# Streaming both halves of x as one 512-column operand in the recurrent block's weight slots

## Chip, core and metric

The kernel runs on one core of one Trainium2 chip. The metric is the device time of one execution in microseconds; the kernel before takes 2019.62 us (median of 3 runs, 2018.29 to 2022.55). The engines are TensorE (PE, its weight loads shown as PEld), VectorE (DVE), ScalarE (ACT), GpSimd (POOL) and SyncE (SP), which issues the transfers. Each works through its own instructions in order and they meet only at semaphores.

## The reference, cut to what matters

Two layers of one kind follow a first block; the change lies in the first block's recurrent part, where x is 256 tokens by 2048 features and `w_in` has 2048 columns for `u_lru` and 2048 for `g_lru`.

```python
xn = rms_norm(x, norm_pre_w[l])
z = xn @ w_in[l]
u_lru, g_lru, q, k, v, g_attn, m_lru, m_attn = jnp.split(z, split_at, axis=-1)
u = centred_depthwise_conv(u_lru, conv_w[l], conv_b[l])      # 4 taps along the tokens
h = rg_lru(u, ..., False) + rg_lru(u, ..., True)
y_a = h * jax.nn.silu(g_lru)

def rg_lru(u, w_r, b_r, w_i, b_i, lam, reverse):             # 16 blocks of 128 features
    gate_r = sigmoid(einsum(u, w_r) + b_r)
    gate_i = sigmoid(einsum(u, w_i) + b_i)
    log_a = -LRU_C * gate_r * softplus(-lam)
    a = exp(log_a)
    b = sqrt(-expm1(2.0 * log_a)) * (gate_i * u)
    return associative_scan over tokens of h = a * h + b
```

## The kernel before

All matrices arrive as "slots" of 128 x 2048 numbers (1 MB each). A slot n passes three stages in the class `Ring`: SP loads it into one of two raw buffers (`load`, L251), ACT rounds it to the short format fp32r (`round`, L260, the instruction at L267), DVE subtracts the rounded from the raw weights to get the residual (`residual`, L269, the instruction at L274). `w_hi` and `w_lo` have four places each. A raw buffer is loaded anew once the residual of the slot that held it is done; a place of `w_hi` is overwritten once PE has counted the slot as `used`. x is likewise held as `xn_hi` and `xn_lo`. A product is three matmuls: hi·hi, lo·hi and hi·lo.

Slots 0 to 31 are the recurrent part. `features` (L294) multiplies one slot, that is 128 output features over all 2048 inputs: for each of 16 rows kk it issues three matmuls with 256 moving columns (the tokens), 48 in all, adding up in the left half of one of the four PSUM banks `z0` to `z3`. The pass i (L1107 to L1117) takes slots 4i and 4i+1 (two tiles of u, banks 0 and 1), slots 4i+2 and 4i+3 (two tiles of g, banks 2 and 3), and then `gates(i)` (L1095), the 8 small products of the gate matrices with the convolved u. There are 8 passes. Slots 32 to 39 follow (keys and values, `tokens`, L306, with 512 moving columns), then the attention part.

Beside PE, ACT and DVE each run a loop that is written out by hand (ACT L599 to L627, DVE L859 to L888). Its iteration i serves the gates and the scan of pass i-1 and the convolution of pass i. With n = 4i:

- ACT: `gate_inputs(i-1)` takes the sigmoid of the two g tiles from PSUM (L555), `gates(i-1)` takes 8 sigmoids of the gate products (L563, L565), then round n+3, 4 tanh (L575), round n+4, two `input_copy` of u out of PSUM into `padded` (L593), 4 exp (L582), a square root (L585), rounds n+5 and n+6, and `round_y` (L597), which waits for DVE's y.
- DVE: `open_gates(i-1)` (L829: g times its sigmoid, from PSUM), residual n+3, residual n+4, `convolve` of two tiles (each L818 and three of L822, each waiting for the one before), the scan (L835 to L844), residual n+5, `outputs_lru` (L849 and L852, the instruction that writes y), residual n+6 and `split_y` (L856).
- POOL multiplies gate_i by u (L509) as soon as the 8 sigmoids are done.

PE starts a u slot of pass i when `input_copy` of pass i-1 has emptied its bank (`ucopied`), a g slot when `open_gates` of pass i-1 has (`zcopied`), and `gates(i)` when both convolutions of pass i are done (`conv`). In iteration 0 DVE works through a chain of small instructions for the angles and for softplus (L163 to L173, L892 to L896) before it comes to `open_gates(0)`.

Of the kernel before, what the change touches and what calls it, by code (L numbers as in the profile page):

```python
# [10 lines left out]
F32R = mybir.dt.float32r  # L11
I32 = mybir.dt.int32
ACT = mybir.ActivationFunctionType
ALU = mybir.AluOpType
AX_X = mybir.AxisListType.X

P = 128
D = 2048
T = 256
KT = D // P  # L20
# [4 lines left out]
SLOTS = 4  # L25
# [6 lines left out]
LRU_PASSES = KT // 2  # L32
# [211 lines left out]
class Ring:  # L244
# [49 lines left out]
    def features(self, pe, n, out, x_hi, x_lo, each=None, whole=True):  # L294
# [8 lines left out]
                ins = pe.matmul(out, w[:, kk], x[:, kk], start=kk == 0 and j == 0, stop=kk == KT - 1 and j == 2)  # L303
        ins.then_inc(self.s.used, 1)

    def tokens(self, pe, n, quarter, outs, x_hi, x_lo):  # L306

        w_hi, w_lo = (w[:, n % SLOTS].rearrange("p (k f) -> p k f", k=4) for w in (self.k.w_hi, self.k.w_lo))
        self.await_slot(pe, n)
        for kk in range(4):  # L310
            row = 4 * quarter + kk
            for m in range(2):
                t = slice(P * m, P * m + P)
                for j, (x, w) in enumerate(((x_hi, w_hi), (x_hi, w_lo), (x_lo, w_hi))):
                    ins = pe.matmul(outs[m], x[:, row, t], w[:, kk], start=row == 0 and j == 0, stop=row == KT - 1 and j == 2)  # L315
        ins.then_inc(self.s.used, 1)
# [26 lines left out]
def reduce_angles(link, dve, angle, turns, rest, looked):  # L343
# [4 lines left out]
    for n, quarter in enumerate((0.0, 0.25)):  # L348
# [5 lines left out]
        for m, part in enumerate(turn_parts):  # L354
# [5 lines left out]

B1_SEMS = ("loaded0 loaded1 rounded split used "
           "p1_in ident_in consts_in x0 x1 x2 x3 eps squared averaged rooted first0 first1 first2 first_rounded first_split scaled ascaled turned xrounded xsplit "
           "weights0 weights1 gated cleared chain exped ucopied conv gsig zcopied gates taken decay dsteps rounded_y ydone "
           "counted rotary_in rchain rlooked mask_in sink_in sinkready "
           "kcopied kroped kturned keyed vcopied qcopied roped qturned qevac scored0 scored1 soft0 soft1 "
           "exped0 exped1 flipped0 flipped1 fcopied0 fcopied1 mixed0 mixed1 yout0 yout1 yrounded0 yrounded1 ylo silued "
# [4 lines left out]
def first_block(k, t):  # L371

    nc = k.nc
    z, aux = k.z, k.aux
    with phase(nc, "b1", B1_SEMS) as s:
        put, goto = k.put, k.goto
        ring = Ring(k, s, 0, 0, SLOTS_1 + SLOTS - 1)
# [6 lines left out]
        padded = put("padded", [P, 2, T + 4])  # L384
        gsig, g_all, y = put("gsig", [P, 2, T]), put("g_all", [P, 2, T]), put("y", [P, 2, T])
        gate_r, gate_i, decay, tau = (put(n, [P, 2, 2, T]) for n in ("gate_r", "gate_i", "decay", "tau"))
# [47 lines left out]
        soft, exped = (s.soft0, s.soft1), (s.exped0, s.exped1)  # L434
# [5 lines left out]

        def tile(n):
            return z[n][:, 0:T]

        def pair(c):
            return (z[2 * (c % 2)][:, 0:Q], z[2 * (c % 2) + 1][:, 0:Q])
# [10 lines left out]
        with nc.Block() as block:  # L456
# [55 lines left out]
            def _(act):  # L512
# [34 lines left out]
                ring.round(act, 1)  # L547
                ring.round(act, 2)

                def gate_inputs(i):  # L550
                    act.wait_ge(s.used, 4 * i + 4)
                    if i:
                        act.wait_ge(s.zcopied, 2 * i)
                    for b in range(2):
                        act.activation(gsig[:, b], tile(2 + b), ACT.Sigmoid).then_inc(s.gsig, 1)  # L555

                def gates(i):
                    if i:
# [40 lines left out]
                for i in range(LRU_PASSES + 1):  # L599
                    n = 4 * i  # L600
                    if i:
                        gate_inputs(i - 1)
                        gates(i - 1)
                    ring.round(act, n + 3)
                    if i:
                        tanhs(i - 1)
                    ring.round(act, n + 4)
                    if i < LRU_PASSES:
                        input_copy(i, 0)
                        input_copy(i, 1)  # L610
                    if i:
                        exps_lru(i - 1)
                    else:
                        act.wait_ge(s.chain, 2)
                        act.activation(tmp[1][:], tmp[0][:], ACT.Exp).then_inc(s.exped, 1)
                    ring.round(act, n + 5)
                    if i == 0:

                        act.wait_ge(s.rchain, RCHAIN_1 + 8)
                        act.activation(sin_1[:, :, 0:16], rest_1[:, :, 0:16], ACT.Sin, scale=-1.0).then_inc(s.rlooked, 1)  # L620
                        act.activation(sin_1[:, :, 16:32], rest_1[:, :, 16:32], ACT.Sin).then_inc(s.rlooked, 1)
                    ring.round(act, n + 6)
                    if i == 0:
                        act.wait_ge(s.rchain, RCHAIN_1 + 16)
                        act.activation(cos_1[:], rest_1[:], ACT.Sin).then_inc(s.rlooked, 1)
                    if i:
                        round_y(i - 1)  # L627
# [141 lines left out]
            def _(dve):  # L769
# [41 lines left out]

                def convolve(i, b):
                    dve.wait_ge(s.ucopied, 2 * i + b + 1)
                    u = u_all[:, 2 * i + b:2 * i + b + 1]
                    for tap in range(4):
                        x = padded[:, b, tap:tap + T]
                        if tap == 0:
                            ins = dve.tensor_scalar(u, x[:, None], col(P1_CONV, 2 * i + b), col(P1_CONVB, 2 * i + b),  # L818
                                                    ALU.mult, ALU.add)
                        else:  # L820
                            dve.wait_ge(s.conv, 8 * i + 4 * b + tap)
                            ins = dve.scalar_tensor_tensor(out=u, in0=x[:, None], scalar=col(P1_CONV + 16 * tap, 2 * i + b),  # L822
                                                           in1=u, op0=ALU.mult, op1=ALU.add)
                        ins.then_inc(s.conv, 1)

                def open_gates(i):
                    dve.wait_ge(s.gsig, 2 * i + 2)
                    for b in range(2):
                        dve.tensor_tensor(g_all[:, b], tile(2 + b), gsig[:, b], ALU.mult).then_inc(s.zcopied, 1)  # L829

                def scan(i):
                    def step(n):
# [26 lines left out]
                for i in range(LRU_PASSES + 1):  # L859
                    n = 4 * i  # L860
                    if i:
                        open_gates(i - 1)
                    ring.residual(dve, n + 3)
                    if i == 0:
                        link = chain(dve, s.chain)
                        link(lambda: dve.tensor_scalar(rate[:], params[:, P1_LAM:P1_LAM + 32], -1.0, None, ALU.mult))
# [203 lines left out]
            def _(pe):  # L1070
# [36 lines left out]
                for i in range(LRU_PASSES):  # L1107
                    for b in range(2):
                        if i:
                            pe.wait_ge(s.ucopied, 2 * (i - 1) + b + 1)  # L1110
                        first = i == b == 0
                        ring.features(pe, 4 * i + b, tile(b), k.xn_hi, k.xn_lo, first_rows if first else None, not first)
                    for b in range(2):
                        if i:
                            pe.wait_ge(s.zcopied, 2 * (i - 1) + b + 1)
                        ring.features(pe, 4 * i + 2 + b, tile(2 + b), k.xn_hi, k.xn_lo)
                    gates(i)  # L1117

                pe.wait_ge(s.ucopied, 2 * LRU_PASSES)
                for w in range(4):  # L1120
                    ring.tokens(pe, SLOT_K + w, w, pair(0), k.xn_hi, k.xn_lo)

# [7 lines left out]
                        if h % 2:  # L1130
                            ins.then_inc(out_sem, 1)

                pe.wait_ge(s.zcopied, 2 * LRU_PASSES)
                for w in range(4):
                    ring.tokens(pe, SLOT_V + w, w, pair(1), k.xn_hi, k.xn_lo)
                    if w == 1:
# [1704 lines left out]
def build(nc, t):  # L2841

    with ExitStack() as stack:
# [17 lines left out]
        k.cos_t, k.sin_t = put("cos_t", [P, T]), put("sin_t", [P, T])  # L2861
        k.xn_at = SBUF_END - 8 * KT * T
        k.middle = goto(k.xn_at)
        k.xn_hi, k.xn_lo = (put(n, [P, KT, T], F32R) for n in ("xn_hi", "xn_lo"))
        goto(k.xn_at)
        k.junk = put("junk", [P, D])
        goto(k.xn_at + 4 * KT * T)
# [107 lines left out]
```

## Time and profile before

| what | value |
|---|---|
| median of 3 runs | 2019.62 us |
| the profiled execution | 2015.25 us |
| its span (first to last instruction) | 2013.5 us |
| PE busy in the span | 1942.0 us |
| DVE busy | 1265.4 us |
| ACT busy | 1099.0 us |
| granted TensorE clock, mean | 0.990 |

The profiled execution is 4.37 us below the median and 1.75 us longer than its span. Each row of a timeline gives the start, the duration, the engine, the line, the operation with its output and inputs, and, in brackets, the idle time of the engine before it with what ended it. Rows of one line that follow each other are merged (x4). Matmuls overlap in their records, so their pace is read from the distance of the starts and not from the durations.

### The profile page before, as it was taken

Reading aid. Unit: us, or ns where it says so; the run is one execution under the profiler, and the core shown is the slowest. Engines: PE = TensorE matmul, PEld = TensorE weight load, DVE = VectorE, ACT = ScalarE, POOL = GpSimd, SP = SyncE. Lnnn points to the kernel's source line nnn. Section 1 sums busy time; section 2 is a strip of 40 time slices with the busy share of each in tenths; the row PEclk is TensorE's granted clock in tenths of the full one; section 3 lists DMA queues with packets and bytes.
Section 4 is the critical chain, followed back from the end, with each engine's and each line's share of the span. In section 5 each row is a group of like instructions: output and inputs, shape, how many; then the busy total and the mean of one; then the engine's idle time right before and its main releaser. Section 6 shows DMA issues by size and latency. Waiting matters only on the chain. (4 is left out here: it accounts for less than half of the span.)

```text
span 2013.5 us, 32797 instructions
## 1 busy us (share of the span) xinstructions
PE 1942.0 (96%) x13840; PEld 1731.8 (86%) x13840; DVE 1265.4 (63%) x1768; ACT 1099.0 (55%) x1499; POOL 70.0 (3%) x66
## 2 busy tenths in 40 slices
PE   6999999999999999999999999999989998999998
PEld 6999989999888888887898988888879998998886
DVE  5877755555444444654697878554547889765453
ACT  5877745554433333334655579626454656883451
POOL 0111100000000000000000101100000000010000
PEclk9999999999999999999999999999999999999999
DMA  6455454444455555464644333313655443342153
GB/s 219 186 189 186 152 205 162 160 147 147 167 189 194 194 182 201 173 249 146 236 163 174 135 129 126 126 65 126 212 185 197 178 147 126 126 147 85 65 208 127
DMA packets 52274, 328.63 MB, mean 163 GB/s; under 512 B 7968, under 2 KB 10144, under 8 KB 14368
## 3 DMA queue, kind: packets, MB, share of 16 engines
q1 hardware_dynamic: 52128, 326.54, 45.0%
q8 instruction: 109, 1.79, 0.3%
q14 instruction: 37, 0.30, 0.0%
HBM read 320.23 MB, written 6.29 MB: 162 GB/s over the span
## 5 line engine op out<-in xcount | busy, mean ns | idle before, releaser
L274 DVE TENSOR_TENSOR w_lo<-w_raw,w_hi 128x2048 fp32r<-128x2048 f32 x275 | 633.6, 2305 | 439.9 <-ACT w_hi L267 439.7
L267 ACT ACTIVATE w_hi<-w_raw 128x2048 fp32r<-128x2048 f32 x287 | 549.5, 1917 | 514.0 <-PE z L315 249.6
L303 PE MATMUL z<-xn_hi,w_hi 128*128 128x256 f32 x2112 | 621.0, 294 | 4.3 <-DVE w_lo L274 2.9
L303 PE MATMUL z<-xn_hi,w_lo 128*128 128x256 f32 x2112 | 598.0, 283 | 0.0
L303 PE MATMUL z<-xn_lo,w_hi 128*128 128x256 f32 x2112 | 597.4, 283 | 0.0
L303 PEld LDWEIGHTS z<-xn_hi,w_hi 128*128 128x128 f32 x2112 | 401.5, 190 | 20.7 <-issue 9.3
L303 PEld LDWEIGHTS z<-xn_lo,w_hi 128*128 128x128 f32 x2112 | 400.3, 190 | 5.1 <-issue 4.3
L303 PEld LDWEIGHTS z<-xn_hi,w_lo 128*128 128x128 f32 x2112 | 398.7, 189 | 0.0
L315 PE MATMUL z<-w_hi,xn_hi 128*128 128x512 f32 x568 | 226.9, 399 | 0.0
L315 PE MATMUL z<-w_lo,xn_hi 128*128 128x512 f32 x568 | 225.2, 396 | 0.0
L315 PE MATMUL z<-w_hi,xn_lo 128*128 128x512 f32 x568 | 225.1, 396 | 0.0
L315 PE MATMUL z<-w_hi,y_hi 128*128 128x512 f32 x368 | 143.6, 390 | 0.0
L315 PE MATMUL z<-w_hi,y_lo 128*128 128x512 f32 x368 | 143.3, 389 | 0.0
L315 PE MATMUL z<-w_lo,y_hi 128*128 128x512 f32 x368 | 143.2, 389 | 0.0
L315 PEld LDWEIGHTS z<-w_hi,xn_lo 128*128 128x128 f32 x568 | 107.0, 188 | 26.1
L315 PEld LDWEIGHTS z<-w_hi,xn_hi 128*128 128x128 f32 x568 | 107.0, 188 | 25.4
L315 PEld LDWEIGHTS z<-w_lo,xn_hi 128*128 128x128 f32 x568 | 107.0, 188 | 25.3
L1963 DVE SCALAR_TENSOR_TENSOR acc<-padded_b,params,acc 128x256 f32<-128x256 f32 x240 | 98.4, 478 | 0.0
L315 PEld LDWEIGHTS z<-w_hi,y_lo 128*128 128x128 f32 x368 | 69.1, 188 | 14.5
L315 PEld LDWEIGHTS z<-w_hi,y_hi 128*128 128x128 f32 x368 | 69.1, 188 | 14.1
L315 PEld LDWEIGHTS z<-w_lo,y_hi 128*128 128x128 f32 x368 | 69.1, 188 | 14.1
L2121 DVE SCALAR_TENSOR_TENSOR conv<-padded,params,conv 128x256 f32<-128x256 f32 x108 | 58.1, 538 | 35.2 <-ACT conv L1692 32.6
(425 smaller groups left out, 2525.0 us busy)
## 6 DMA issues: line engine op xcount, KB each, us to landing
w_raw<-in_w_dram SPq DMA_DIRECT2D x287, 1024.0 KB, 4.8
gate_w<-in_lru_w_dram SPq DMA_DIRECT2D x8, 512.0 KB, 5.3
x_t<-state_dram SPq DMA_DIRECT2D x2, 2048.0 KB, 7.8
x_first<-in_x_dram SPq DMA_DIRECT2D x4, 512.0 KB, 6.7
x_t<-in_x_dram SPq DMA_DIRECT2D x1, 2048.0 KB, 10.9
state_dram<-x_t SPq DMA_DIRECT2D x2, 1024.0 KB, 5.3
pw<-in_pw_dram SPq DMA_DIRECT2D x2, 1024.0 KB, 6.2
state_dram<-x_t SPq DMA_DIRECT2D x8, 256.0 KB, 2.1
```

The source lines that it names most:

```text
L267: act.activation(self.k.w_hi[:, n % SLOTS], self.k.w_raw[:, m % RAW], ACT.Copy).then_inc(self.s.rounded, 1)
L274: dve.tensor_tensor(self.k.w_lo[:, n % SLOTS], self.k.w_raw[:, m % RAW], self.k.w_hi[:, n % SLOTS].bitcast(F32), ALU.subtract).then_inc(se ...
L303: ins = pe.matmul(out, w[:, kk], x[:, kk], start=kk == 0 and j == 0, stop=kk == KT - 1 and j == 2)
L315: ins = pe.matmul(outs[m], x[:, row, t], w[:, kk], start=row == 0 and j == 0, stop=row == KT - 1 and j == 2)
L1963: dve.scalar_tensor_tensor(out=acc[:, b], in0=padded_b[:, b, n:n + T], scalar=col(w), in1=acc[:, b], op0=ALU.mult, op1=ALU.add).then_inc(s ...
L2121: dve.scalar_tensor_tensor(out=conv[:, i], in0=padded[:, i, tap:tap + T], scalar=col(w), in1=conv[:, i], op0=ALU.mult, op1=ALU.add).then_i ...
```

## The change

The 32 slots use a new function `wide_features`. `xn_hi` and `xn_lo` are now two halves of one tensor `xn` of shape [128, 2, 16, 256]. For each row kk, `w_hi` is loaded once and multiplied with both halves of x as one moving operand of 512 columns (two runs of 256), giving hi·hi in the left half of the bank and lo·hi in the right half; `w_lo` with `xn_hi` is added to the left half. A slot has 32 matmuls where it had 48. The sum of the halves is made outside: ACT copies the left half to SBUF, DVE adds the right half from PSUM. For u the copy is the `input_copy` that was there and the addition is new in `convolve`; for g the copy (`take_gates`) and the addition (`join_gates`) are both new, and the sigmoid and the product with it now read `g_all` in SBUF. PE waits for the additions (`ujoined`, `gjoined`) instead of `ucopied` and `zcopied`.

```diff
+    def wide_features(self, pe, n, out, x, each=None, whole=True):
+        w_hi, w_lo = (w[:, n % SLOTS].rearrange("p (k f) -> p k f", k=KT) for w in (self.k.w_hi, self.k.w_lo))
+        parts = out[:, 0:2 * T].rearrange("p (b t) -> p b t", b=2)
+        if whole:
+            self.await_slot(pe, n)
+        for kk in range(KT):
+            if each is not None:
+                each(kk)
+            if kk < KT - 1:
+                pe.matmul(parts, w_hi[:, kk], x[:, :, kk], start=kk == 0, stop=False)
+            ins = pe.matmul(out[:, 0:T], w_lo[:, kk], x[:, 0, kk], start=False, stop=False)
+            if kk == KT - 1:
+                ins = pe.matmul(parts, w_hi[:, kk], x[:, :, kk], start=False, stop=True)
+        ins.then_inc(self.s.used, 1)
...
+                def take_gates(i):
+                    act.wait_ge(s.used, 4 * i + 4)
+                    if i:
+                        act.wait_ge(s.dsteps, 8 * i)
+                    for b in range(2):
+                        act.activation(g_all[:, b], tile(2 + b), ACT.Copy).then_inc(s.gtaken, 1)
                 def gate_inputs(i):
-                    act.wait_ge(s.used, 4 * i + 4)
...
-                        act.activation(gsig[:, b], tile(2 + b), ACT.Sigmoid).then_inc(s.gsig, 1)
+                        act.wait_ge(s.gjoined, 2 * i + b + 1)
+                        act.activation(gsig[:, b], g_all[:, b], ACT.Sigmoid).then_inc(s.gsig, 1)
...
                     if i:
+                        take_gates(i - 1)
+                        gates(i - 1)
                         gate_inputs(i - 1)
-                        gates(i - 1)
                     ring.round(act, n + 3)
...
                 def convolve(i, b):
                     dve.wait_ge(s.ucopied, 2 * i + b + 1)
+                    inner = padded[:, b, 2:2 + T]
+                    dve.tensor_tensor(inner, rest(b), inner, ALU.add).then_inc(s.ujoined, 1)
+                    dve.wait_ge(s.ujoined, 2 * i + b + 1)
...
+                def join_gates(i):
+                    for b in range(2):
+                        dve.wait_ge(s.gtaken, 2 * i + b + 1)
+                        dve.tensor_tensor(g_all[:, b], rest(2 + b), g_all[:, b], ALU.add).then_inc(s.gjoined, 1)
...
                     if i:
+                        join_gates(i - 1)
+                    ring.residual(dve, n + 3)
+                    if i:
                         open_gates(i - 1)
-                    ring.residual(dve, n + 3)
...
                         if i:
-                            pe.wait_ge(s.ucopied, 2 * (i - 1) + b + 1)
+                            pe.wait_ge(s.ujoined, 2 * (i - 1) + b + 1)
                         first = i == b == 0
-                        ring.features(pe, 4 * i + b, tile(b), k.xn_hi, k.xn_lo, first_rows if first else None, not first)
+                        ring.wide_features(pe, 4 * i + b, z[b], k.xn, first_rows if first else None, not first)
```

On PE, within a slot of pass 1, the rows were:

```order
L1103 MATMUL aux<-u_all,gate_w_85 128x256 x8
L303 MATMUL z<-xn_hi,w_hi 128x256
L303 MATMUL z<-xn_lo,w_hi 128x256
L303 MATMUL z<-xn_hi,w_lo 128x256
L303 MATMUL z<-xn_hi,w_hi 128x256
```

(the number behind a name is its buffer's) and are now, at the end of one slot and the start of the next:

```order
L316 MATMUL z<-xn,w_hi 128x512
L317 MATMUL z<-xn,w_lo 128x256 x2
L319 MATMUL z<-xn,w_hi 128x512
L316 MATMUL z<-xn,w_hi 128x512
L317 MATMUL z<-xn,w_lo 128x256
```

Two matmuls of 256 columns on the same weights have become one of 512; in the last row the order of the two is turned round.

On DVE, one iteration from y to the scan (L274 is a residual, L829 `open_gates`, L818 and L822 `convolve`) was:

```order
L852 TENSOR_TENSOR y<-gate_r,g_all 128x512
L274 TENSOR_TENSOR w_lo<-w_raw,w_hi 128x2048
L856 TENSOR_TENSOR y_lo<-y,y_hi 128x512
L829 TENSOR_TENSOR g_all<-z,gsig 128x256 x2
L274 TENSOR_TENSOR w_lo<-w_raw,w_hi 128x2048 x2
L818 TENSOR_SCALAR u_all<-padded,params 128x256
L822 SCALAR_TENSOR_TENSOR u_all<-padded,params,u_all 128x256 x3
L818 TENSOR_SCALAR u_all<-padded,params 128x256
L822 SCALAR_TENSOR_TENSOR u_all<-padded,params,u_all 128x256 x3
```

and is now (L859 `join_gates`, L865 `open_gates`, L842 the addition in `convolve`):

```order
L888 TENSOR_TENSOR y<-gate_r,g_all 128x512
L274 TENSOR_TENSOR w_lo<-w_raw,w_hi 128x2048
L892 TENSOR_TENSOR y_lo<-y,y_hi 128x512
L859 TENSOR_TENSOR g_all<-z,g_all 128x256 x2
L274 TENSOR_TENSOR w_lo<-w_raw,w_hi 128x2048
L865 TENSOR_TENSOR g_all<-g_all,gsig 128x256 x2
L274 TENSOR_TENSOR w_lo<-w_raw,w_hi 128x2048
L842 TENSOR_TENSOR padded<-z,padded 128x256
L848 TENSOR_SCALAR u_all<-padded,params 128x256
L852 SCALAR_TENSOR_TENSOR u_all<-padded,params,u_all 128x256 x3
L842 TENSOR_TENSOR padded<-z,padded 128x256
L848 TENSOR_SCALAR u_all<-padded,params 128x256
```

Four instructions of 256 columns are added, and `open_gates` has moved behind residual n+3.

On ACT, from `round_y` to round n+3 (L267), the rows were:

```order
L597 ACTIVATE y_hi<-y 128x512
L555 ACT_TABLE_LOAD
L555 ACTIVATE gsig<-z 128x256 x2
L563 ACTIVATE gate_r<-aux,params 128x256
L565 ACTIVATE gate_i<-aux,params 128x256
```

and are now:

```order
L623 ACTIVATE y_hi<-y 128x512
L574 ACTIVATE g_all<-z 128x256 x2
L589 ACT_TABLE_LOAD
L589 ACTIVATE gate_r<-aux,params 128x256
```

The two copies are added, and the two `gsig` (now L581) have moved behind the 8 sigmoids, ahead of round n+3.

## Rows read from the trace of the kernel before

**Rows 1.** The page: busy time of the engines.
```profile
PE 1942.0 (96%) x13840; PEld 1731.8 (86%) x13840; DVE 1265.4 (63%) x1768; ACT 1099.0 (55%) x1499; POOL 70.0 (3%) x66
```

**Rows 2.** Timeline of PE, slot 31 into gates(7): start, duration, instruction.
```profile
227.83 0.29 PE L303 MATMUL z<-xn_hi,w_lo 128*128 128x256 f32 x1
...
233.71 2.54 PE L1103 MATMUL aux<-u_all,gate_w 128*128 128x256 f32 x11
```

**Rows 3.** Timeline of PE, a stretch of 512-column matmuls.
```profile
699.79 0.39 PE L315 MATMUL z<-w_hi,xn_hi 128*128 128x512 f32 x1
...
705.88 0.40 PE L315 MATMUL z<-w_hi,xn_lo 128*128 128x512 f32 x1
```

**Rows 4.** Timeline of PE: gates(1), gates(2).
```profile
74.78 3.62 PE L1103 MATMUL aux<-u_all,gate_w 128*128 128x256 f32 x16
...
101.28 3.62 PE L1103 MATMUL aux<-u_all,gate_w 128*128 128x256 f32 x16
```

**Rows 5.** Timeline of DVE, iteration 3.
```profile
105.25 0.69 DVE L852 TENSOR_TENSOR y<-gate_r,g_all 128x512 f32<-128x512 f32 x1
...
113.33 2.94 DVE L274 TENSOR_TENSOR w_lo<-w_raw,w_hi 128x2048 fp32r<-128x2048 f32 x1 [3.91 <-ACT w_hi L267]
116.72 2.29 DVE L274 TENSOR_TENSOR w_lo<-w_raw,w_hi 128x2048 fp32r<-128x2048 f32 x1 [0.45 <-ACT w_hi L267]
118.93 0.41 DVE L818 TENSOR_SCALAR u_all<-padded,params 128x256 f32<-128x256 f32 x1
119.38 1.52 DVE L822 SCALAR_TENSOR_TENSOR u_all<-padded,params,u_all 128x256 f32<-128x256 f32 x3
...
122.70 1.22 DVE L835 SCALAR_TENSOR_TENSOR tau<-decay,tau 128x1024 f32<-128x1024 f32 x1
...
126.41 0.67 DVE L842 TENSOR_TENSOR_SCAN gate_r<-decay,tau 128x256 f32<-128x256 f32 x1
...
130.55 0.69 DVE L852 TENSOR_TENSOR y<-gate_r,g_all 128x512 f32<-128x512 f32 x1
```

**Rows 6.** Timeline of ACT, iteration 3.
```profile
105.98 0.63 ACT L597 ACTIVATE y_hi<-y 128x512 fp32r<-128x512 f32 x1 [4.35 <-DVE y L852]
...
114.72 1.97 ACT L267 ACTIVATE w_hi<-w_raw 128x2048 fp32r<-128x2048 f32 x1
...
121.57 1.06 ACT L585 ACTIVATE tau<-tau 128x1024 f32<-128x1024 f32 x1
```

**Rows 7.** Timeline of POOL, same iteration.
```profile
111.57 2.55 POOL L509 TENSOR_TENSOR gate_i<-gate_i,u_all 128x512 f32<-128x512 f32 x2 [22.74 <-ACT gate_i L565]
```

**Rows 8.** Timelines of ACT and DVE, iteration 1.
```profile
66.01 0.62 ACT L593 ACTIVATE padded<-z 128x256 f32<-128x256 f32 x2
66.65 1.28 ACT L582 ACT_TABLE_LOAD   x1
...
62.69 0.75 DVE L829 TENSOR_TENSOR g_all<-z,gsig 128x256 f32<-128x256 f32 x2
63.35 2.28 DVE L274 TENSOR_TENSOR w_lo<-w_raw,w_hi 128x2048 fp32r<-128x2048 f32 x1
```

**Rows 9.** Timeline of PE: three idle stretches, in brackets.
```profile
27.11 0.58 PE L303 MATMUL z<-xn_hi,w_hi 128*128 128x256 f32 x1 [2.89 <-DVE w_lo L274]
...
63.16 0.38 PE L303 MATMUL z<-xn_hi,w_hi 128*128 128x256 f32 x1 [0.90 <-DVE g_all L829]
...
1157.29 0.33 PE L2518 MATMUL aux<-ident,S 128*128 128x128 f32 x1 [2.06 <-DVE S L2102]
```

**Rows 10.** Windows: PE, PEld, DVE, ACT, POOL busy; granted clock; DMA share, GB/s.
```profile
30.00:33.00 3.00, 3.00 (x16) 3.00 (x15) 1.08 (x1) 0.00 (x0) 0.00 (x0) 0.50 0.86 350
1155.00:1160.00 5.00, 2.94 (x19) 1.73 (x19) 2.53 (x9) 4.97 (x8) 0.00 (x0) 1.00 0.54 203
```

**Rows 11.** Timeline of DVE, iterations 7 and 8.
```profile
236.05 0.69 DVE L852 TENSOR_TENSOR y<-gate_r,g_all 128x512 f32<-128x512 f32 x1
...
257.80 2.27 DVE L274 TENSOR_TENSOR w_lo<-w_raw,w_hi 128x2048 fp32r<-128x2048 f32 x1
```

More of the change, by code:

```diff
@@ L362 @@
            "p1_in ident_in consts_in x0 x1 x2 x3 eps squared averaged rooted first0 first1 first2 first_rounded first_split scaled ascaled turned xrounded xsplit "
-           "weights0 weights1 gated cleared chain exped ucopied conv gsig zcopied gates taken decay dsteps rounded_y ydone "
+           "weights0 weights1 gated cleared chain exped ucopied ujoined conv gtaken gjoined gsig zcopied gates taken decay dsteps rounded_y ydone "
            "counted rotary_in rchain rlooked mask_in sink_in sinkready "
@@ L442, in tile, with rest @@
             return z[n][:, 0:T]
+        def rest(n):
+            return z[n][:, T:2 * T]
         def pair(c):
@@ L824, in convolve @@
                         ins.then_inc(s.conv, 1)
+                def join_gates(i):
+                    for b in range(2):
+                        dve.wait_ge(s.gtaken, 2 * i + b + 1)
+                        dve.tensor_tensor(g_all[:, b], rest(2 + b), g_all[:, b], ALU.add).then_inc(s.gjoined, 1)
                 def open_gates(i):
                     dve.wait_ge(s.gsig, 2 * i + 2)
+                    dve.wait_ge(s.gjoined, 2 * i + 2)
                     for b in range(2):
-                        dve.tensor_tensor(g_all[:, b], tile(2 + b), gsig[:, b], ALU.mult).then_inc(s.zcopied, 1)
+                        dve.tensor_tensor(g_all[:, b], g_all[:, b], gsig[:, b], ALU.mult).then_inc(s.zcopied, 1)
                 def scan(i):
@@ L1109, in _ @@
                         if i:
-                            pe.wait_ge(s.ucopied, 2 * (i - 1) + b + 1)
+                            pe.wait_ge(s.ujoined, 2 * (i - 1) + b + 1)
                         first = i == b == 0
-                        ring.features(pe, 4 * i + b, tile(b), k.xn_hi, k.xn_lo, first_rows if first else None, not first)
+                        ring.wide_features(pe, 4 * i + b, z[b], k.xn, first_rows if first else None, not first)
                     for b in range(2):
                         if i:
-                            pe.wait_ge(s.zcopied, 2 * (i - 1) + b + 1)
-                        ring.features(pe, 4 * i + 2 + b, tile(2 + b), k.xn_hi, k.xn_lo)
+                            pe.wait_ge(s.gjoined, 2 * (i - 1) + b + 1)
+                        ring.wide_features(pe, 4 * i + 2 + b, z[2 + b], k.xn)
                     gates(i)
-                pe.wait_ge(s.ucopied, 2 * LRU_PASSES)
+                pe.wait_ge(s.ujoined, 2 * LRU_PASSES)
                 for w in range(4):
@@ L1131, in turn_heads @@
                             ins.then_inc(out_sem, 1)
-                pe.wait_ge(s.zcopied, 2 * LRU_PASSES)
+                pe.wait_ge(s.gjoined, 2 * LRU_PASSES)
                 for w in range(4):
@@ L2863, in build @@
         k.middle = goto(k.xn_at)
-        k.xn_hi, k.xn_lo = (put(n, [P, KT, T], F32R) for n in ("xn_hi", "xn_lo"))
+        k.xn = put("xn", [P, 2, KT, T], F32R)
+        k.xn_hi, k.xn_lo = k.xn[:, 0], k.xn[:, 1]
         goto(k.xn_at)
```

## The prediction

> **What bounds the kernel now.** I read the page first: PE is busy in 96% of the span [rows 1], so what counts is its pace and its few waits. From 227.83 to 233.71 PE starts 49 matmuls of 256 columns, one per 0.1200 us, so a slot of 48 takes 5.76 us [rows 2]. With 512 columns 26 starts take 6.09 us, 0.2342 us each [rows 3]. gates(1) and gates(2) start 26.50 us apart [rows 4]; less 4 x 5.76 that leaves 3.45 us for the gate products. In the passes after the first PE has one idle stretch, 0.90 us at slot 6 [rows 9]. So PE bounds the stage. Before pricing anything I looked at how much room ACT and DVE have behind it, because the change gives both of them work.
>
> They have less than their busy shares suggest, because they form a loop. DVE writes y; ACT has waited for it (4.35 us idle), does round_y, the gate sigmoids and round n+3; DVE has waited for that (3.91 us idle), and then works almost without a pause through two residuals, the convolutions, the scan and residual n+5 to the next y [rows 5, 6]. From y to y this takes 130.55 - 105.25 = 25.30 us, and nothing in it waits for PE. That is 1.2 us less than PE's pass. The loop started late (softplus in iteration 0) and gains 1.2 us per pass until it meets PE: y of iteration 7 comes at 236.05 [rows 11], 26.4 us per pass after that of iteration 3, PE's own pace.
>
> **The change part by part.**
>
> *PE.* A wide slot has 16 x 0.2342 + 16 x 0.1200 = 5.667 us against 5.760: 0.093 us less. The number of streamed columns is the same (768 per row kk); all that goes is what a matmul costs beyond its columns, 2 x 0.1200 - 0.2342 = 0.0058 us, 16 times. Slot 0 is fed row by row by x and slot 1 runs largely at half clock, where there is nothing to win if the two sizes scale with the columns; 30 slots give 2.8 us. A pass becomes 4 x 5.667 + 3.45 = 26.12 us. Bounds: the wide operand has two runs of 256 columns, which no row shows; at worst it costs two matmuls (0.240, nothing saved). At best the whole 0.0133 us per small matmul above 256 columns at 2.4 GHz (0.1067) is a fixed price paid once: 0.2267, 0.21 us per slot, 6.4 us. I take 0.2342, the measured operand of that size.
>
> By the Trainium skill (TensorE: Matmul & The Clock Gate, back-to-back rates of a warm array) a matmul starts N/2.4 + 2.5 ns after the one before, which would make the saving an estimated 16 x 2.5 = 40 ns per slot; the rows are at 120 and 234 ns where the rule has 109 and 216, so the trace does not agree.
>
> *The ACT/DVE loop, what it gains in length.* (a) The two copies of take_gates stand on the chain from y to round n+3. Two such copies cost 66.65 - 66.01 = 0.64 us [rows 8]. The two gsig only change places within that chain. So round n+3 and everything behind it on ACT is 0.64 later. (b) join_gates falls into DVE's 3.91 us of idle: nothing. (c) open_gates now stands between the two residuals, about 0.66 us on DVE (62.69 to 63.35 in [rows 8]). Residual n+3 took 2.94 us where the next took 2.29; POOL runs from 111.57 to 114.12 [rows 7] and residual n+3 starts at 113.33, inside. Now it starts 0.64 later against POOL, at 113.97, and nearly all of the 0.65 of stretching goes. It ends at about 116.36 as before (116.27), open_gates reaches 117.02, and residual n+4 waits for ACT's round n+4 anyway: 114.72 + 0.64 + 2.00 = 117.36, against 116.72. So (a) to (c) together move residual n+4 by 0.64. If the stretching stayed, DVE would be the later one, by 0.15: that is the bound above. (d) Each convolution gets an addition that its first tap waits for. The nearest row is L818, same width, waited for by the next: 119.38 - 118.93 = 0.45; read from PSUM, L829 has 0.33 for each of an unchained pair [rows 8]. I take 0.44, 0.88 for two. Bounds: 0.33 and the scan's 0.67 [rows 5]. The square root that the scan needs ended at 122.63 with the scan at 122.70 [rows 5, 6]; it moves by 0.64, the scan by 1.52, so nothing is added there. The loop becomes 25.30 + 0.64 + 0.88 = 26.82 us.
>
> The Trainium skill (SBUF, who interferes with whom) calls the port pair of VectorE and GpSimd an exclusive lock against which a two-input VectorE instruction fully blocks; the 2.94 us of residual n+3 agrees with that.
>
> So the loop, now faster than PE by 1.2 us per pass, becomes slower than PE by 0.7. The rest is a matter of where each starts.
>
> *Where they meet.* In iteration 0 the two additions delay DVE by 0.88; its chain up to the sinks, and so join_gates(0), starts at 62.69 + 0.88 = 63.57. PE may start slot 6 when the first addition is done, about 64.03 instead of 63.16. PE would be there at 62.26 - 4 x 0.093 = 61.88, so it idles 2.15 us instead of 0.90: 1.25 us lost. Two wide slots later gates(1) is at 64.03 + 11.33 + 0.1 = 75.46 (before: 74.78). Residual 7 starts at 63.35 + 0.88 = 64.23 [rows 8], takes 2.2, open_gates 0.66, so residual 8 starts at 67.1. From there to the scan, which starts as the convolutions end, it was 122.70 - 116.72 = 5.98 [rows 5], now 6.86: they end at 74.0, ahead of PE by 1.5. From here DVE's end of the convolutions runs at 26.82 per pass: 100.8, 127.6, 154.5, 181.3, 208.1, 234.9. PE at 26.12 asks for gates(2) at 101.6, gates(3) at 127.7 and gates(4) at 153.8. From gates(4) on PE waits, about 0.7 us in each of four passes. gates(7) starts at 235.0 against 233.71 [rows 2]: 1.3 us later.
>
> *Behind the stage.* DVE goes into the key and value slots late. y of iteration 7 came at 236.05, 7.85 us behind the scan's start, and moves to 242.7 (+6.7); residual n+5 of iteration 8, slot 37, ended at 257.80 + 2.27 = 260.07 [rows 11] and moves by 6.7 + 0.64 to 267.4. PE wants slot 37 at 235.0 + 3.45 + 5 x 24 x 0.2342 = 266.5. It waits 0.9 us; the key transposes behind slot 37 may add 0.1. After that ACT and DVE have little beside the weights, and the ring catches up; the shift of PE reaches the end, since PE stays the bound.
>
> *The sum.* -2.8 (30 slots) + 1.25 (slot 6) + 4 x 0.7 (gates) + 1.0 (slot 37) = +2.25, less roundings: +2.2 us. The profiled execution of 2015.25 would become 2017.5; against the median of 2019.62 that is 2021.8 us.
>
> **Rivals.**
>
> *A. PE bounds throughout, not slower than before.* The loop stays at or below 26.1, because the additions pipeline (0.33 each) and the copies hide: 25.30 + 0.66 = 25.96. For: DVE still idles 3.9 us per pass. Against: that idle time is a wait inside the loop, not room. Price: -2.8 + 1.2 at slot 6, -1.6: 2018.0 us.
>
> *B. Slower by over 0.2%: the additions in convolve cost as much as the scan's 0.67.* They read PSUM and write in place over data that the tap waits for. Each is then 0.23 dearer, 0.46 per pass, counted in iteration 0 and in six loops: +3.2 on top of +2.2, so 2025.0 us. It decides from 0.57 us per addition (1.8 us / 14 more). Against: L818, also waited for, has 0.45. Late weight transfers in the lengthened loop would look alike.
>
> *C. The wide matmul saves nothing (0.240).* PE's pass stays at 26.49 and gates(1) comes at 75.65, then PE is at 234.6 for gates(7), still before the loop's 235.0. The time is the forecast's, 2021.8: from pass 4 on the loop decides, and the pace of the matmul does not matter. For the same reason the best case of 0.2267 gains only at the start, under 1 us.
>
> *D. The idle 2.15 us at slot 6 lowers the clock.* After 2.89 us of idle the granted clock was 0.50 at 30 to 33 us, the 1.2 GHz level [rows 9, 10]. After 2.06 us at 1157 the window around it is granted 1.00. If it falls as it did then (27.11 to 33, 5.9 us at half pace), PE loses some 3 us at slots 6 and 7, but the loop is behind by then and gates(7) is still set by it: under 0.5 us more. The sum stays.
>
> **How the numbers follow.** Forecast, with C and D (they end at the same time): 0.68. A: 0.10. B or a like lengthening: 0.18. Something that makes both PE and the loop faster: 0.04. What a measurement of this kernel can tell from no change is about 0.2%, 4 us. Over 4 us faster needs a gain beyond the best bound of the matmul at an unchanged loop: 0.04. Over 4 us slower is B and the upper end of the forecast: 0.22. Within: 0.74. The range: A with its spread and the runs' scatter of 2 us gives 2017.5 below; B beyond its middle gives 2026.5.
>
> **What would show it.** Wide matmuls start 0.234 apart and the small ones 0.120; y to y is 26.8 us on DVE from iteration 1 on; PE idles 2.1 us before slot 6, nothing before gates(2) and gates(3), 0.7 us before gates(4) to gates(7) (released by u_all, DVE), and 0.9 before slot 37; residual n+3 falls to about 2.3 us. I am wrong if PE has no waits before the gates (then A) or if they exceed 1.2 us each (then B).

## The result, and the profile after

The changed kernel takes 2023.67 us (median of 22 runs, 2019.98 to 2030.24) against 2019.95 us for the kernel before (22 runs, 2015.33 to 2023.40). The ratio is 1.0021, 95% interval 1.0014 to 1.0029: 4.2 us slower, between 2.8 and 5.9 (the two medians alone differ by 3.7). The profiled execution took 2022.95 us and has a span of 2020.9. The forecast was 2.2 us slower. The direction and the length of the loop came out; the size was about half of what was measured, because a wait at the start of the stage was overlooked.

First the starts of the gate products on PE in the changed kernel, and PE's waits around them (start, duration, instruction; in brackets the idle time and what ended it; the same instructions as in [rows 4] and [rows 9]):

```profile
46.42 3.72 PE L1141 MATMUL aux<-u_all,gate_w 128*128 128x256 f32 x16 [0.40 <-DVE u_all L852]
63.93 0.50 PE L316 MATMUL z<-xn,w_hi 128*128 128x512 f32 x1 [2.57 <-DVE g_all L859]
76.94 3.72 PE L1141 MATMUL aux<-u_all,gate_w 128*128 128x256 f32 x16
103.77 3.72 PE L1141 MATMUL aux<-u_all,gate_w 128*128 128x256 f32 x16 [0.67 <-DVE u_all L852]
130.60 3.72 PE L1141 MATMUL aux<-u_all,gate_w 128*128 128x256 f32 x16 [0.68 <-DVE u_all L852]
...
237.93 3.72 PE L1141 MATMUL aux<-u_all,gate_w 128*128 128x256 f32 x16 [0.68 <-DVE u_all L852]
270.32 0.50 PE L331 MATMUL z<-w_hi,xn 128*128 128x512 f32 x1 [0.56 <-DVE w_lo L274]
```

From gates(2) on, and not only from gates(4) as forecast, PE waits in every pass for the second convolution, and the gates come 26.83 us apart where they came 26.49 apart. gates(7) is at 237.93 instead of 233.71. Next DVE, one iteration of its loop (the rows that answer to [rows 5]):

```profile
111.47 0.69 DVE L888 TENSOR_TENSOR y<-gate_r,g_all 128x512 f32<-128x512 f32 x1
...
120.17 2.34 DVE L274 TENSOR_TENSOR w_lo<-w_raw,w_hi 128x2048 fp32r<-128x2048 f32 x1 [4.53 <-ACT w_hi L267]
122.43 0.75 DVE L865 TENSOR_TENSOR g_all<-g_all,gsig 128x256 f32<-128x256 f32 x2
123.56 2.29 DVE L274 TENSOR_TENSOR w_lo<-w_raw,w_hi 128x2048 fp32r<-128x2048 f32 x1 [0.38 <-ACT w_hi L267]
125.77 0.42 DVE L842 TENSOR_TENSOR padded<-z,padded 128x256 f32<-128x256 f32 x1
126.22 0.41 DVE L848 TENSOR_SCALAR u_all<-padded,params 128x256 f32<-128x256 f32 x1
...
130.46 1.22 DVE L871 SCALAR_TENSOR_TENSOR tau<-decay,tau 128x1024 f32<-128x1024 f32 x1
```

y of the next iteration starts at 138.30, 26.83 after this one. An addition costs 126.22 - 125.77 = 0.45 us. Residual n+3 takes 2.34 us and no longer 2.94, and open_gates fits into the wait ahead of the next residual. The loop is the forecast's to 0.01 us.

Then the place where the forecast did not hold. ACT in iteration 1, the wait for the gate additions:

```profile
63.91 0.75 ACT L581 ACTIVATE gsig<-g_all 128x256 f32<-128x256 f32 x2 [5.29 <-DVE g_all L859]
64.57 1.90 ACT L267 ACTIVATE w_hi<-w_raw 128x2048 fp32r<-128x2048 f32 x1
```

ACT has finished its 8 sigmoids at 58.6 and stands idle for 5.29 us, because gsig needs the joined g, and join_gates(0) on DVE comes at 63.46, behind the softplus chain. Round 7, which stands behind gsig, starts at 64.57. Residual 7 on DVE starts at 66.49 instead of the forecast's 64.23.

Last the pace of the matmuls within a wide slot of the changed kernel:

```profile
108.03 0.39 PE L316 MATMUL z<-xn,w_hi 128*128 128x512 f32 x1
108.26 0.28 PE L317 MATMUL z<-xn,w_lo 128*128 128x256 f32 x1
108.38 0.39 PE L316 MATMUL z<-xn,w_hi 128*128 128x512 f32 x1
...
110.83 0.39 PE L316 MATMUL z<-xn,w_hi 128*128 128x512 f32 x1
```

Seven rows kk (110.83 less 108.38) take 2.45 us, 0.350 each: 0.23 for the wide matmul and 0.12 for the small one. A slot of 16 rows takes 5.60 us, 0.16 less than before, where the forecast had 0.09.

### The profile page after: what moved, and what is told of

Its sections match the earlier page's. It is cut to its first block and busy times, and to the rows that moved or that the text cites. A ratio compares the mean times of both kernels' runs of the same rounds, so it can differ in the third digit from the quotient of the medians.

```text
span 2020.9 us, 31839 instructions
## 1 busy us (share of the span) xinstructions
PE 1942.5 (96%) x13328; PEld 1706.0 (84%) x13328; DVE 1273.9 (63%) x1800; ACT 1103.7 (55%) x1515; POOL 70.4 (3%) x66
## 5 line engine op out<-in xcount | busy, mean ns | idle before, releaser
L274 DVE TENSOR_TENSOR w_lo<-w_raw,w_hi 128x2048 fp32r<-128x2048 f32 x275 | 629.6, 2290 | 442.3 <-ACT w_hi L267 442.0
L267 ACT ACTIVATE w_hi<-w_raw 128x2048 fp32r<-128x2048 f32 x287 | 549.0, 1915 | 519.2 <-PE z L331 240.4
L303 PE MATMUL z<-xn,w_hi 128*128 128x256 f32 x3200 | 606.4, 289 | 1.1 <-DVE xn L232 1.1
L303 PEld LDWEIGHTS z<-xn,w_hi 128*128 128x128 f32 x3200 | 497.8, 190 | 22.2 <-issue 14.2
L303 PE MATMUL z<-xn,w_lo 128*128 128x256 f32 x1600 | 452.4, 283 | 0.0
L331 PE MATMUL z<-w_hi,xn 128*128 128x512 f32 x1136 | 363.5, 398 | 0.6 <-DVE w_lo L274 0.6
L303 PEld LDWEIGHTS z<-xn,w_lo 128*128 128x128 f32 x1600 | 301.4, 188 | 0.0
L331 PEld LDWEIGHTS z<-w_hi,xn 128*128 128x128 f32 x1136 | 214.0, 188 | 52.4 <-DVE w_lo L274 1.0
L331 PE MATMUL z<-w_lo,xn 128*128 128x512 f32 x568 | 225.2, 396 | 0.0
L316 PE MATMUL z<-xn,w_hi 128*128 128x512 f32 x480 | 176.0, 405 | 5.4 <-DVE w_lo L274 2.9
L317 PE MATMUL z<-xn,w_lo 128*128 128x256 f32 x512 | 139.3, 282 | 0.0
L331 PEld LDWEIGHTS z<-w_lo,xn 128*128 128x128 f32 x568 | 107.0, 188 | 25.3
L316 PEld LDWEIGHTS z<-xn,w_hi 128*128 128x128 f32 x480 | 91.7, 191 | 26.5 <-DVE w_lo L274 3.2
L317 PEld LDWEIGHTS z<-xn,w_lo 128*128 128x128 f32 x512 | 97.9, 191 | 2.7
```

Source lines behind the costliest of these rows:

```text
L267: act.activation(self.k.w_hi[:, n % SLOTS], self.k.w_raw[:, m % RAW], ACT.Copy).then_inc(self.s.rounded, 1)
L274: dve.tensor_tensor(self.k.w_lo[:, n % SLOTS], self.k.w_raw[:, m % RAW], self.k.w_hi[:, n % SLOTS].bitcast(F32), ALU.subtract).then_inc(se ...
L316: pe.matmul(parts, w_hi[:, kk], x[:, :, kk], start=kk == 0, stop=False)
L317: ins = pe.matmul(out[:, 0:T], w_lo[:, kk], x[:, 0, kk], start=False, stop=False)
```

## The experiments

Because the start of the stage differs between profiles (gates(0) lies between 45.5 and 47.4 us, slot 1 starting when its weights are there and running partly at the lower clock), the table gives the distance from gates(0) to gates(7), read like the rows above. In the kernels whose gates(0) waits for DVE (changed, narrow, early_join, early_take, both, and by 0.21 us noadd) this distance starts at DVE's first convolutions; in the kernel before these ended at 45.4 us, and gates(0) came later, at 47.13, for PE's own sake. Ratios are to the kernel before, run anew beside each. The distances come from one profiled execution each, the ratios from all runs. The column of y is the distance of two y on DVE in iterations 1 to 4.

| kernel | gates(0) | gates(1) less gates(0) | gates(7) less gates(0) | y to y | ratio, 95% interval |
|---|---|---|---|---|---|
| before | 47.13 | 27.65 | 186.58 | 25.30 | 1 |
| changed | 46.42 | 30.52 | 191.51 | 26.83 | 1.0021 (1.0014 to 1.0029) |
| narrow | 47.41 | 30.51 | 191.45 | 26.82 | 1.0014 (1.0005 to 1.0023) |
| noadd | 45.63 | 30.59 | 185.91 | 25.30 | 0.9985 (0.9975 to 0.9995) |
| early_join | 47.28 | 28.20 | 189.19 | 26.83 | 1.0010 (1.0001 to 1.0019) |
| early_take | 46.85 | 30.51 | 190.22 | 26.28 | 1.0007 (0.9997 to 1.0016) |
| both | 47.15 | 28.20 | 185.86 | 26.28 | 1.0000 (0.9990 to 1.0010) |
| weave_only | 46.29 | 28.97 | 184.41 | 25.88 | 0.9988 (0.9979 to 0.9997) |
| woven | 45.48 | 26.75 | 182.18 | 25.33 | 0.9967 (0.9956 to 0.9977) |
| narrow_woven | 46.96 | 26.44 | 185.06 | 25.33 | 0.9976 (0.9967 to 0.9985) |

(From y of iteration 3 to that of 4 it is 26.04 in the kernel before and 26.54 in noadd; the other early intervals of these two are 25.30. In the kernel before, ACT there waits 0.68 us for PE's u, the first sign of PE's pace in the loop; in noadd it waits 1.13 us for late weights.)

**narrow: the additions without the wide matmul.**

```diff
-            if kk < KT - 1:
-                pe.matmul(parts, w_hi[:, kk], x[:, :, kk], start=kk == 0, stop=False)
+            if kk == 0:
+                pe.matmul(parts, w_hi[:, kk], x[:, :, kk], start=True, stop=False)
+            elif kk < KT - 1:
+                for half in range(2):
+                    pe.matmul(out[:, half * T:half * T + T], w_hi[:, kk], x[:, half, kk], start=False, stop=False)
```

> The changed kernel, but in the 14 inner rows kk of each slot the 512-column matmul is two of 256 columns again (the second into the right half of the bank); copies and additions stay. Theory (from gates(2) on the ACT/DVE loop of 26.83 us sets the pace, not the matmuls): gates(7) starts at 237.9 us as in the changed kernel, PE's waits before the gates shrink from 0.68 to about 0.35 us, y to y stays 26.8, time within 0.5 us of the changed kernel's, 4 to 5 us above before. Rival (matmul pace counts): each pass 0.33 us longer, gates(7) at 240 or later.

The distances are those of the changed kernel (191.45 against 191.51). The ratios, 1.0014 and 1.0021, have overlapping intervals; the time is 2.8 us above before, where 4 to 5 was expected. gates(7) itself lies at 238.86 and not at 237.9, but gates(0) is 1.0 us later in this profile too. No wait above 0.15 us is left before gates(2) to gates(7), where 0.35 was expected. With the loop in charge the pace of PE's matmuls has no effect on the stage.

**noadd: the wide matmul without the additions.**

```diff
-                        ring.features(pe, 4 * i + b, tile(b), k.xn_hi, k.xn_lo, first_rows if first else None, not first)
+                        ring.wide_features(pe, 4 * i + b, z[b], k.xn, first_rows if first else None, not first)
...
-                        ring.features(pe, 4 * i + 2 + b, tile(2 + b), k.xn_hi, k.xn_lo)
+                        ring.wide_features(pe, 4 * i + 2 + b, z[2 + b], k.xn)
```

> The kernel before with wide_features alone: the right half of the bank (x_lo times w_hi) is computed but never added, that part of the sum is left out; ACT and DVE do exactly what they did before. Theory: the loop stays at 25.3 us, PE bounds again with a pass of 26.12, gates(7) at about 231.3 against 233.71 before, the time 2.4 us (0.12%) below before. Rival (the wide operand with its two runs saves nothing): gates(7) at 233.7. Rival (the clock or the start of the stage makes the changed kernel late, not the additions): gates(7) stays near 237.

gates(7) at 231.54, the time 3.0 us below before (interval 1 to 5). PE bounds, and its pass is 25.88 us: more is saved than forecast. PE idled 2.78 us before slot 6, since it reached it sooner than DVE had emptied the bank. Behind it the granted clock fell to the 1.2 GHz level for a while (0.84 from 60 to 66 us, 0.88 from 66 to 72), and two slots took 12.88 us (63.34 to 76.22) instead of 11.2: 1.7 us lost. This wait and this clock make the 30.59 in the table, not the overlooked wait of the changed kernel. So the matmul alone would have been a gain, and the copies and additions turn it into a loss.

**early_join: the first gate additions ahead of softplus.**

```diff
-                    if i:
+                    if i > 1:
                         join_gates(i - 1)
...
                     else:
+                        join_gates(0)
                         dve.wait_ge(s.exped, 1)
                         softplus_tail(...)
```

> The changed kernel, with the two additions of join_gates(0) on DVE in iteration 0 ahead of the softplus chain instead of behind it. Theory (the part that the prediction missed: in iteration 1 ACT's gsig, and behind it round 7, wait for join_gates(0), which stands behind softplus): PE does not wait before slot 6 (2.57 us in the changed kernel), no half clock behind it, round 7 on ACT starts near 59.3 instead of 64.6, the convolutions of pass 1 end near 74.4 instead of 76.9, and all gates come 2.5 us earlier, gates(7) at 235.4; y to y stays 26.83; the time 2.5 us below the changed kernel, 1.5 to 2.5 us above before. Rival (only the clock drop behind slot 6 counts): gates(1) is earlier but gates(7) stays at 237.9, because the loop decides it.

PE no longer waits before slot 6, round 7 on ACT starts at 59.92, and gates(1) comes 28.20 us behind gates(0) instead of 30.52: 2.3 us, as the theory of the missed wait has it. y to y stays at 26.83. The distance to gates(7) falls by the same 2.3 us to 189.19, which the rival excluded. gates(7) itself is at 236.47 and not at 235.4, because this profile's gates(0) is 0.9 us later. The ratio falls from 1.0021 to 1.0010, their intervals overlapping.

One thing was not expected: PE's wait is not gone but has moved to gates(1), and the clock fell behind it after all (0.79 from 72 to 78 us); the gate products take 5.41 us where they take 3.72 elsewhere.

```profile
75.48 5.41 PE L1142 MATMUL aux<-u_all,gate_w 128*128 128x256 f32 x16 [2.06 <-DVE u_all L852]
```

At gates(7) this costs nothing: 75.48 + 6 x 26.83 = 236.46, the loop's own place.

**early_take: the copies of g off the chain.** g_all becomes two buffers (`g_two[i % 2]`), and the copies move into ACT's wait for y (the rest of the edit follows from the two buffers):

```diff
                     if i:
-                        take_gates(i - 1)
                         gates(i - 1)
...
+                    if i < LRU_PASSES:
+                        take_gates(i)
                     if i:
                         round_y(i - 1)
```

> The changed kernel with the double buffered g_all and the two copies ahead of round_y, but join_gates(0) left behind the softplus chain. Theory (two separate terms: the late start of iteration 1 and the loop's length): the wait before slot 6 stays near 2.6 us and gates(1) near 76.9, y to y is 26.28; PE waits 0.35 us before the gates from gates(2) or (3) on; gates(7) minus gates(0) is 191.5 - 6 x 0.55 = 188.2 us; the time 2.5 to 3 us below the changed kernel. Rival (moving the copies also removes the late start): gates(1) near 75.

y to y is 26.28, the copies are worth 0.55 us of the loop, and gates(1) stays at 30.51: two separate terms. The ratio, 1.0007 (0.9997 to 1.0016), puts the time 2.8 us below the changed kernel, as expected, though the ends of the two intervals overlap. The last two intervals of y in this profile are 27.48 and 27.10, and the distance to gates(7) is 190.2 where 188.2 was expected. ACT stands there for late weights (last column: the releaser, a transfer):

```profile
200.98 1.92 ACT L267 ACTIVATE w_hi<-w_raw 128x2048 fp32r<-128x2048 f32 x1 [1.09 <-DMA w_raw<-in_w_dram]
...
228.09 1.91 ACT L267 ACTIVATE w_hi<-w_raw 128x2048 fp32r<-128x2048 f32 x1 [0.71 <-DMA w_raw<-in_w_dram]
```

The two intervals are 1.20 and 0.82 us longer than 26.28, at waits of 1.09 and 0.71. When the loop sets the pace, a late transfer costs its whole delay.

**both: early_join and early_take.**

> early_join, and g_all in two buffers so that ACT's two copies of g (take_gates) stand ahead of round_y, in ACT's wait for y, and no longer on the chain from y to round n+3. Theory (the copies are 0.64 us of the loop's 26.83): y to y is 26.2 us, PE waits under 0.15 us before each of the gates, gates(7) at 231.5, slot 37 at 263.2, the time 2 us (0.1%) below before. Rival (the additions alone make the loop, the copies were hidden): y to y stays 26.8, gates(7) at 235.4.

y to y is 26.28, 0.1 more than expected. The distance to gates(7) is 0.7 us below before, and the time is that of before (ratio between 0.9990 and 1.0010), not 2 us below. PE's wait has moved to gates(1), as in early_join, and its clock fell behind it. The windows (busy times of PE, PEld, DVE, ACT and POOL, granted clock, DMA):

```profile
75.35 5.41 PE L1144 MATMUL aux<-u_all,gate_w 128*128 128x256 f32 x16 [2.05 <-DVE u_all L854]
...
72.00:78.00 6.00, 3.95 (x17) 3.14 (x16) 5.75 (x10) 5.99 (x6) 0.00 (x0) 0.89 0.41 164
78.00:84.00 6.00, 6.00 (x28) 5.03 (x27) 5.90 (x8) 0.56 (x3) 0.00 (x0) 0.82 0.04 11
```

gates(2) comes 27.68 us behind gates(1), 1.8 us above the pass of 25.88 that follows. It is tempting to put the missing 2 us down to this, but at gates(7) the drop has cost nothing: PE's passes are shorter than the loop, so it caught up, and 75.35 + 6 x 26.28 = 233.03 is where gates(7) is found (233.01). All y are 26.28 apart, so DVE never waited for PE. The gain over the kernel before is small because the loop, 26.28, is only 0.2 us per pass shorter than the pass of 26.49 before, and gates(1) comes 0.55 us later than before.

**woven: both, with the two convolutions alternating on DVE.**

The code is shortened, words in brackets stand for instructions; ACT's copies of u also wait now for both convolutions of the pass before.

```diff
+                def convolve(i):
+                    for b in range(2):
+                        (addition of tile b)
+                    for tap in range(4):
+                        for b in range(2):
+                            (wait for the tap before of tile b, tap of tile b)
```

> both, and on DVE the additions and taps of the two convolutions of a pass alternate between the tiles, so that no instruction waits for the one directly ahead of it. Theory (the loop of 26.28 us in both still held PE at gates(1), 2.05 us, and from gates(7) on; 10 instructions at about 0.46 become 10 at about 0.38): y to y would be 25.4 us by itself and is PE's pass of 25.9 where PE holds it, the wait at gates(1) falls to about 1.2 us, too short for a clock drop behind it, gates(1) at 74.4, gates(7) minus gates(0) at about 183 us (before: 186.6, changed kernel: 191.5); the time 3 us (0.15%) below before. Rival (PE sets the pace already in both, what is lost there is its clock behind an idle stretch of any length): gates(7) minus gates(0) stays at 185.9 and the time at that of before.

DVE, the same stretch as above:

```profile
119.05 0.75 DVE L845 TENSOR_TENSOR padded<-z,padded 128x256 f32<-128x256 f32 x2
119.72 0.73 DVE L852 TENSOR_SCALAR u_all<-padded,params 128x256 f32<-128x256 f32 x2
120.36 2.46 DVE L856 SCALAR_TENSOR_TENSOR u_all<-padded,params,u_all 128x256 f32<-128x256 f32 x6
122.79 1.22 DVE L875 SCALAR_TENSOR_TENSOR tau<-decay,tau 128x1024 f32<-128x1024 f32 x1
```

Ten instructions now take 3.74 us (119.05 to 122.79), 0.37 each; chained, as in the changed kernel, the same ten take 4.69 (125.77 to 130.46). The loop is 25.33 us, that of before, with all the additions in it. PE waits once, 0.70 us at gates(1) where 1.2 was expected, its clock stays up (1.00 from 60 to 84 us), and from gates(1) on it bounds: 72.23 + 6 x 25.88 = 227.5, measured 227.66. (How short a wait must be to leave the clock up is shown by no run.)

```profile
72.23 3.72 PE L1145 MATMUL aux<-u_all,gate_w 128*128 128x256 f32 x16 [0.70 <-DVE u_all L856]
98.22 3.62 PE L1145 MATMUL aux<-u_all,gate_w 128*128 128x256 f32 x16
...
227.66 3.62 PE L1145 MATMUL aux<-u_all,gate_w 128*128 128x256 f32 x16
```

This version beats both kernels: ratio 0.9967 (0.9956 to 0.9977), 6.7 us below before. The stage from gates(0) to gates(7) explains 4.4 us of that; 1.65 us more lies in this profile ahead of gates(0) (45.48 against 47.13), where the lower clock at slot 1 lasted less long (0.96 from 30 to 33 us, against 0.50 before). Whether that part is the change's or a matter of the profile is not settled; narrow_woven, with the same order on DVE, has gates(0) at 46.96.

**narrow_woven: is it PE in woven?** woven with the matmuls of narrow.

> woven, with the matmuls of narrow (in the 14 inner rows of a slot two matmuls of 256 columns for the one of 512). Theory (in woven PE sets the pace, so here, unlike in narrow, the pace of the matmuls counts): a row kk takes 0.36 instead of 0.35 us, the pass grows from 25.88 to 26.4 us, gates(7) minus gates(0) from 182.2 to 185.5 us, the time 3.5 to 4 us above woven and 2 to 3 us below before. Rival (woven's gain comes from the woven DVE order and the earlier start and not from PE): gates(7) minus gates(0) stays at 182 to 183.

185.06 against woven's 182.18, and the pass is 26.44 us against 25.88 while y to y is 25.33 in both: the slower matmul costs 2.9 us on the stage. The same edit that was without effect on the distances of the changed kernel counts here. The times do not show it by themselves: 0.9976 against 0.9967, 1.8 us where 3.5 to 4 was expected, with overlapping intervals. The time is 4.8 us below before, more than the 1.5 us that the stage gives; where the rest lies was not traced.

**weave_only: the chained additions alone.** The changed kernel with woven's convolve.

> The changed kernel with the woven additions and taps alone: join_gates(0) stays behind softplus and the copies of g stay on the chain. Theory (chained additions and taps are one separable term of the loop): y to y falls from 26.83 by 0.95 to 25.9 us, about PE's own pass; the wait before slot 6 stays at 2 us or more, gates(1) stays late (gates(1) minus gates(0) 29.7 instead of 30.5), gates(7) minus gates(0) is 185 us against 191.5 in the changed kernel and 186.6 before; the time 2 us or less from that of before. Rival (the copies and the start of iteration 1 hold the loop whatever DVE does): y to y stays above 26.3.

y to y is 25.88, equal to PE's own pass; gates(7) less gates(0) is 184.41; the time is 2.4 us below before (ratio 0.9988). The loop and the distance to gates(7) came as expected (25.9 and 185); gates(1), 28.97 us behind gates(0), is 0.7 earlier than expected. Of the three repairs this one is worth most, 0.95 us in each pass, as it is from `both` to `woven` (26.28 and 25.33). PE idled 2.12 us before slot 6 here, longer than the 2.05 before gates(1) in the run `both`, and yet the clock stayed up:

```profile
63.25 0.50 PE L316 MATMUL z<-xn,w_hi 128*128 128x512 f32 x1 [2.12 <-DVE g_all L861]
...
66.00:72.00 6.00, 6.00 (x35) 5.19 (x35) 5.55 (x6) 5.97 (x11) 0.00 (x0) 1.00 0.42 156
```

## Why the prediction was right, and what it missed

**The loop.** 26.82 us predicted, 26.83 measured, and its terms one by one: the addition 0.44 against 0.45; the stretching of residual n+3 gone (2.34 us); open_gates hidden; join_gates in DVE's idle time. Along DVE's rows, from y to residual n+4 it takes 12.09 us and not 11.47, from there to the scan 6.90 and not 5.98: 0.62 for the copies, where 0.64 was put, and 0.92 for the additions, where 0.88 was put. These are the whole 1.53 us between the 25.30 of noadd and the 26.83. early_take, which moved the copies away, got 0.55 of the 0.62 back; the other 0.07 is not traced. That the loop sets the gates' times, and that rival C ends where the forecast does, was shown by narrow. (One slip in the working changed nothing: with residual n+3 still stretched DVE would have been later by 113.97 + 2.94 + 0.66 - 117.36 = 0.21 us, not 0.15.)

**Rivals A and B.** A is out: PE waits before every gate from gates(2) on, and y to y is 26.83. The measured 4.2 us is a size that the prediction kept for B and the upper end of the forecast, but B's reason is out too: an addition costs 0.45 us and not 0.57 or more. The 2 us above the forecast are the next point's.

**The start of iteration 1: this step failed.** The prediction said of gsig that the two "only change places within that chain" and set residual 7 at 64.23. The order of gsig is without effect only from iteration 2 on. In iteration 1 the additions that gsig waits for stand on DVE behind softplus, so the change had added a wait, and behind the waiting gsig stood round 7 and all of DVE's next iteration. The convolutions of pass 1 ended at 76.89 instead of 74.0, and gates(1) came at 76.94 instead of 75.46. The prediction followed join_gates(0) to PE (slot 6, 64.03 predicted, 63.93 measured) and not to ACT. early_join took the wait away and gave back 2.3 of these 2.9 us; the other 0.6 is not assigned to a wait by any run. As the loop starts from there, the 2.9 us went undiminished to gates(7): 237.93 against 235.0. For the same reason PE waited from gates(2) on and not from gates(4).

**PE's pace.** 0.35 us per row kk and not 0.354, a pass of 25.88 and not 26.12 (noadd, woven). The prediction took its 0.2342 from [rows 3]; the trace of the kernel before has the same kind of matmul at another pace too, 13 starts in 2.96 us, 0.228 each:

```profile
1930.41 0.39 PE L315 MATMUL z<-w_hi,y_hi 128*128 128x512 f32 x1
...
1933.37 0.39 PE L315 MATMUL z<-w_lo,y_hi 128*128 128x512 f32 x1
```

In the changed kernel this changed nothing, as the prediction said it would; it is part of why woven gains more than the 2.8 us of the forecast's term.

**The clock (D).** It fell behind slot 6 after 2.57 us of idle (0.90 from 60 to 66 us, 0.82 from 66 to 72), which was held possible, and cost nothing: early_take kept its clock there (1.00 from 60 to 84 us) and has gates(1) at the same 30.51 us behind gates(0).

**Behind the stage.** Slot 37 did wait, 0.56 us where 0.9 was forecast. From then on the shift is carried along: the second layer's first transposes, before and then after, 5.09 us apart.

```profile
958.16 2.77 PE L2425 MATMUL aux<-ident,x_t 128*128 128x128 f32 x10 [6.43 <-DVE x_t L1908]
```
```profile
963.25 2.76 PE L2463 MATMUL aux<-ident,x_t 128*128 128x128 f32 x10 [6.43 <-DVE x_t L1946]
```

**The sum.** Predicted: +1.3 at gates(7), +1.0 at slot 37. Measured: gates(0) 0.71 earlier, gates(1) 2.87 later relative to it, six passes of 26.83 against 26.49 another 2.06: +4.22; then 0.87 more up to the second layer. The remaining 2.3 us between 5.1 and the 7.4 of the two spans grew in the second and third layers, where the kernels are alike. The 22 runs give 4.2 us, so it is a matter of the two profiled executions: that of the kernel before, 2015.25 us, is faster than all of its 22 runs. Most of it goes with the granted clock. Around 1490 us it is 0.83 over 20 us before and 0.74 after, around 1830 us 0.93 over 25 us and 0.86, and across these two places the distance between like instructions of the two kernels grows from 5.4 to 6.3 and from 6.7 to 7.7 us. No experiment was made on it.

## What to carry to other kernels

An engine's idle time is room only if it isn't a wait inside a loop with another engine: work out the loop's length, compare it with the pass of the engine that bounds, and then follow the first pass by itself, where the phases have not settled. A wait that the change adds has to be followed into every engine that takes it, not only into the one that is expected to suffer. Where short chained instructions make up the loop, alternating two independent chains can give more than moving work off the chain: here 0.95 us per pass against 0.55. And a drop of the clock in one profile is not yet a cost: see first whether PE is the one that the others wait for.

## What the runs showed of the hardware

- A VectorE instruction of 256 columns that waits for the one directly ahead of it starts 0.45 to 0.48 us behind it; with another chain's instruction in between, starts are 0.37 us apart on average (4.69 us against 3.74 us for the same ten).
- Matmuls of 512 columns on fp32r operands start their successor after 0.234 us in a row of their kind at 700 us and after 0.228 at 1930 us (kernel before), and after 0.23 when one of 256 columns on other weights follows; 256 columns take 0.12 in either place. What makes the difference between the two places is open. The two separate runs of the moving operand cost nothing visible.
- TensorE's granted clock fell to 0.50, the 1.2 GHz level, after idle stretches of 2.05 us (both), 2.06 us (early_join), 2.28 us (narrow), 2.57 us (changed kernel) and 2.78 us (noadd), and did not after 2.12 us (weave_only) and 2.54 us (early_take). The length of the stretch alone did not decide it in these runs. One place in the second layer, where the kernels are alike, shows it best: behind the wait of [rows 9] at 1157.29 the clock stayed at 1.00 in the kernel before, behind the same wait in the changed kernel it was 0.61 from 1163 to 1167 us.

```profile
1162.86 0.33 PE L2556 MATMUL aux<-ident,S 128*128 128x128 f32 x1 [2.05 <-DVE S L2140]
...
1163.00:1167.00 4.00, 4.00 (x17) 2.15 (x18) 1.75 (x5) 4.00 (x7) 0.00 (x0) 0.61 0.18 72
```
